# A layer with 32 routed experts: both up products of a quad of experts in a row on TensorE, the neighbours' gather and scatter behind them

## The chip, the core and the metric

The kernel runs on one core of a Trainium2 chip. Times are device microseconds of that core; the time of a kernel is the median of several runs. One further execution was taken by the hardware profiler, and all rows in this document come from such an execution. Its engines are called TensorE (PE in the rows; PEld are its weight loads), VectorE (DVE), ScalarE (ACT), GpSimd (POOL) and SyncE (SP), whose queue issues the loads.

## The reference

One decoder layer for 256 tokens of width 1024, in float32: a mixer (differential attention, an mLSTM, gates and an output projection), then a mixture of experts, then a norm. The change is in the experts, which the reference computes densely:

```python
gate = (one_hot(g_sel, N_GROUPS)[:, :, None] * w_e[:, None, :] * p_grp[:, None, None])
for gi in range(N_GROUPS):                       # 4 groups of 8 experts
    a = jnp.einsum('td,edf->tef', t, w_e1[gi])   # 1024 -> 256
    b = jnp.einsum('td,edf->tef', t, w_e3[gi])   # 1024 -> 256
    hid = jax.nn.silu(a) * b * gate[:, gi, :, None]
    y = y + jnp.einsum('tef,efd->td', hid, w_e2[gi])   # 256 -> 1024
```

Each token has two experts with a gate other than zero. The layer's result is x + gt2 * y, and a norm over it is the output.

## The kernel before, in words

The mixer takes the first 250 us or so. Then comes the expert loop. It works on quads of 4 experts, 8 quads in all (`NQ`), each expert on at most 32 tokens (`CAP`), so that a quad's 4 x 32 token places fill the 128 rows of a matmul's output. The loop body is written for 4 quads (`LOOP`) and runs twice. A second block with the same body would handle experts with more than 32 tokens; it is skipped for these inputs. In the rows a float32 matmul of the program stands as two records, so 32 matmuls are x64.

For each quad TensorE does this (function `quad` of the tensor block, lines 1550 to 1568):
- `up("w1")`, line 1533: four experts side by side in four column groups of the array, into the left half of `up_bank`. It first waits until all four w1 tiles have landed (`arrived`, line 1524).
- `gather(0)`, line 1507: matmuls with a one-hot matrix that pick the tokens of the *next* quad, first half of the 1024 features, into `token_bank`.
- `scatter`, line 1496: adds the *previous* quad's outputs to the four banks of y, by a matrix of gates.
- `gather(1)`, line 1507: the second half of the features, into the same `token_bank`. It waits until the first half is evacuated.
- `up("w3")`, line 1533: the second up product, into the right half of `up_bank`.
- `turn`, lines 1514 and 1517: transposes of the next quad's gate matrix and of this quad's hidden values, into `token_bank` again. It waits for the second half's evacuation (`g_evac`) and for the hidden values (`hid_done`).
- `down`, line 1545: experts 0 and 1, then 2 and 3, each pair waiting for its two w2 tiles.

ScalarE (function `quad` of the scalar block, lines 643 to 647) evacuates the two gathers (`gather_half`, line 639, four activations each, then `g_evac`) and computes the sigmoid of the w1 product (line 647). The sigmoid waits on `used` until all 8 up tiles of the quad are consumed, so until the w3 product is done. VectorE multiplies it with both products (lines 1103 and 1105, `hid_done`), copies the transposes (1108, 1110), scales the output (1114, `o_dve`) and makes the next one-hot matrices (1092, 1095).

The weights come by SyncE's queue in the order of use: four tiles of w1, four of w3, four of w2, each 1 MB, so 12 MB a quad. There are 16 slots (`ring` has 12, the buffers hT, qkT, gm and mqk are four more), numbered in turn. SyncE issues load number m once tile m - 16 is consumed (`used`, incremented by the last matmul on each tile). So w3 of a quad goes to the slots of the quad before's w1, w2 to those of its w3, and w1 to those of w2 two quads before.

After the loop TensorE scatters the last quad's output (line 1496), ScalarE squares (668), VectorE norms (1149), and SyncE stores (376).

Of the kernel before, what the change touches and what calls it, by code (L numbers as in the profile page):

```python
# [20 lines left out]
ACT = mybir.ActivationFunctionType  # L21
# [7 lines left out]
G, E, F = 4, 8, 256  # L29
# [54 lines left out]
UP_UNITS = 8  # L84
QU = len(QUAD_UNITS)
# [50 lines left out]
def build(nc, t, out):  # L136
    with ExitStack() as ctx:
# [3 lines left out]
        def sem(name):  # L141
            return ctx.enter_context(nc.semaphore(name))
# [50 lines left out]
        sig, act_a, hid = tmp[:, 0, 0:F], tmp[:, 0, F:2 * F], tmp[:, 1, 0:F]  # L193
# [32 lines left out]
        def S(name, n=1):  # L226

            if name not in small:
                small[name] = (small_at[0], n)
                small_at[0] += n  # L230
            a, n = small[name]
            return sm[:, a:a + n]
# [21 lines left out]
        def pb(job):  # L254
            return bank[JOB[job] % 8]
# [17 lines left out]
        token_bank, up_bank, out_banks = pb("lg"), pb("gt2b0"), (pb("gt2b1"), pb("rank"))  # L273
# [6 lines left out]
        used = sem("used")  # L280
# [8 lines left out]
        s = {n: sem(n) for n in names}  # L289
# [102 lines left out]
        def _(act):  # L392
# [241 lines left out]
            def gather_half(b, half, count):  # L634

                act.wait_ge(s["g_full"], count)
                for j in range(4):
                    k = 4 * half + j
                    ins = act.activation(xg[:, b, k, :], token_bank[:, j * P:(j + 1) * P], ACT.Identity,  # L639
                                         bias=S("B2", KD)[:, k:k + 1], scale=S("A2", KD)[:, k:k + 1])  # L640
                ins.then_inc(s["g_evac"], 1)

            def quad(it, b):
                gather_half(1 - b, 0, it * 2 + 3)
                gather_half(1 - b, 1, it * 2 + 4)
                act.wait_ge(used, it * QU + UP_UNITS)
                act.activation(sig, up_bank[:, 0:F], ACT.Sigmoid).then_inc(s["sig_r"], 1)  # L647

            gather_half(0, 0, 1)
            gather_half(0, 1, 2)  # L650
            with act.Fori(0, NQ // 2) as i:
                for b in range(2):
                    quad(i * 2 + b, b)
            act.wait_ge(s["flag_r"], 1)
            over = act.value_load(flag[0:1, 0:1], min_val=0, max_val=1)
            with act.If(over > 0):
                with act.Fori(1, PASSES) as p:
                    with act.Fori(0, NQ // 2) as i:
                        for b in range(2):
                            quad(p * NQ + i * 2 + b, b)  # L660
# [493 lines left out]
        def _(pe):  # L1154
# [137 lines left out]
            for h in range(HEADS):  # L1292
                for c in range(2):
                    ps = take(f"s{2 * h + c}")
                    r = slice(64 * c, 64 * c + 64)
# [196 lines left out]
            def scatter(b, stop):  # L1492

                for tt in range(TT):
                    for c in range(2):
                        ins = pe.matmul(y_banks[2 * tt + c][:], ptg[:, b, tt, :], outs2[:, 512 * c:512 * c + 512],  # L1496
                                        start=False, stop=stop, skip_group_check=True)
                    if stop:
                        ins.then_inc(s["y_full"], 1)
                return ins  # L1500

            def gather(half):

                for j in range(4):
                    k = 4 * half + j
                    for tt in range(TT):
                        ins = pe.matmul(token_bank[:, j * P:(j + 1) * P], xn[:, tt, k * P:(k + 1) * P],  # L1507
                                        pone[:, tt].rearrange("p a n -> p (a n)"), start=(tt == 0), stop=(tt == TT - 1))
                ins.then_inc(s["g_full"], 1)

            def turn(with_hidden):

                for tt in range(TT):
                    ins = pe.transpose(token_bank[:, tt * P:(tt + 1) * P], pgate[:, tt].rearrange("p a n -> p (a n)"), ident)  # L1514
                if with_hidden:
                    for f in range(2):
                        ins = pe.transpose(token_bank[:, T + f * P:T + (f + 1) * P], hid[:, f * P:(f + 1) * P], ident)
                ins.then_inc(s["pt_full"], 1)

            def arrived(w, e, r, j):  # L1520

                m = j * QU + QUAD_POS[(w, e)]
                n = NPRE + m % XSLOTS
                pe.wait_ge(landed[slot_of(n)], r * (16 * TURNS) + (landed_value(n) + 16 * (m // XSLOTS)))
                return unit(n, 2 if w == "w2" else 8)

            def up(w, r, j, b):

                half = slice(0, F) if w == "w1" else slice(F, 2 * F)
                wt = [arrived(w, e, r, j) for e in range(QUAD)]  # L1530
                for k in range(KD):
                    for e in range(QUAD):
                        ins = pe.matmul(up_bank[e * CAP:(e + 1) * CAP, half], xg[:, b, k, e * CAP:(e + 1) * CAP],  # L1533
                                        wt[e][:, k, :], start=(k == 0), stop=(k == KD - 1), tile_position=(0, e * CAP))
                        if k == KD - 1:
                            ins.then_inc(used, 1)

            def down(r, j):

                for pair in ((0, 1), (2, 3)):  # L1540
                    wt = {e: arrived("w2", e, r, j) for e in pair}
                    for c in range(2):
                        for f in range(2):
                            for e in pair:
                                ins = pe.matmul(out_banks[c][e * CAP:(e + 1) * CAP, :], hidT[:, f, e * CAP:(e + 1) * CAP],  # L1545
                                                wt[e][:, f, 512 * c:512 * c + 512], start=(f == 0), stop=(f == 1),
                                                tile_position=(0, e * CAP))
                                if c == 1 and f == 1:
                                    ins.then_inc(used, 1)

            def quad(r, j):
                it, b = r * LOOP + j, j % 2
                pe.wait_ge(s["g_evac"], it * 2 + 2)
                pe.wait_ge(s["hid_done"], it + 1)
                up("w1", r, j, b)
                pe.wait_ge(s["pg_ready"], it + 2)
                pe.wait_ge(s["pt_evac"], it + 2)
                gather(0)
                pe.wait_ge(s["o_dve"], it + 1)
                scatter(1 - b, False).then_inc(s["scat"], 1)  # L1560
                pe.wait_ge(s["g_evac"], it * 2 + 3)
                gather(1)
                up("w3", r, j, b)
                pe.wait_ge(s["g_evac"], it * 2 + 4)
                pe.wait_ge(s["hid_done"], it + 2)
                turn(True)
                pe.wait_ge(s["hT_evac"], it + 1)
                down(r, j)
# [22 lines left out]
            with pe.Fori(0, NQ // LOOP) as r:  # L1591
                for j in range(LOOP):
                    quad(r, j)
            pe.wait_ge(s["flag_r"], 1)
            over = pe.value_load(flag[0:1, 0:1], min_val=0, max_val=1)
            with pe.If(over > 0):
                with pe.Fori(1, PASSES) as p:
                    with pe.Fori(0, NQ // LOOP) as r:
                        for j in range(LOOP):
                            quad(p * (NQ // LOOP) + r, j)  # L1600
# [26 lines left out]
```

## Time and profile before

| | us |
|---|---|
| median of 3 timed runs | 538.76 (537.51 to 539.1) |
| span of the profiled execution | 540.9 |
| TensorE busy in it | 442.4 (82%) |
| ScalarE, VectorE, GpSimd busy | 171.8, 161.4, 140.9 |
| mean granted TensorE clock | 0.920 |
| moved by DMA | 163.16 MB, mean 302 GB/s |

The page gives the profiled execution's time as its span, 540.9 us; that is 2.1 us above the median of the timed runs. Busy shares are averages over stages with different limits: GpSimd is busy in the mixer only, and the expert loop begins at 289.5 us, when TensorE starts the first w1 product. Of TensorE's busy time, the up products (line 1533) and the down products (line 1545) are the loop's large items.

### The profile page before, as it was taken

What the parts mean: (1) busy time and instruction counts of PE and PEld (TensorE: products, weight loads), DVE (VectorE), ACT (ScalarE), POOL (GpSimd) and SP (SyncE); (2) the same over time, 40 slices, a digit from 0 to 9 for tenths busy, and PEclk for the clock granted to TensorE, in tenths of its full rate; (3) what the DMA queues carried; (4) which work ended last, traced back from release to release, by engine and by line L of the source; (5) the groups of instructions that cost most, each with busy time, mean ns of one, the idle gap of its engine ahead of it and who ended that gap; (6) DMA issues with size and microseconds to landing.
All of it is one profiled execution on the core that took longest, in us unless ns stands there. A gap on an engine that the chain in (4) does not pass through costs nothing.

```text
span 540.9 us, 8837 instructions
## 1 busy us (share of the span) xinstructions
PE 442.4 (82%) x3772; PEld 324.9 (60%) x3772; DVE 161.4 (30%) x338; ACT 171.8 (32%) x305; POOL 140.9 (26%) x36
## 2 busy tenths in 40 slices
PE   2656998999999999979969898969848588385783
PEld 0325988899899999969846453616225153151431
DVE  0245105796464331682360111120111101102013
ACT  3044523743495485433343212301203012030122
POOL 0019663665556559745000000000000000000000
PEclk9857999998999999988989898988979989799898
DMA  8999689396794464579599999999999999999972
GB/s 299 383 370 382 174 270 349 116 366 218 219 355 166 148 229 170 167 260 291 186 397 325 366 376 349 393 350 361 381 348 389 354 355 388 348 383 359 352 293 81
DMA packets 116742, 163.16 MB, mean 302 GB/s; under 512 B 6642, under 2 KB 99044, under 8 KB 116580
## 3 DMA queue, kind: packets, MB, share of 16 engines
q1 hardware_dynamic: 111968, 159.53, 86.0%
q10 hardware_dynamic: 4740, 3.15, 2.1%
q8 instruction: 25, 0.41, 0.3%
q14 instruction: 9, 0.07, 0.0%
HBM read 161.61 MB, written 1.05 MB: 301 GB/s over the span
## 4 chain that ended last, share of the span: by engine, by line
PE 71%; DMA 15%; DVE 7%; ACT 2%; SPq 2%; issue 2%; DVEq 0%
PE bank L1225 32%; PE bank L1533 12%; DMA ring<-in_w_e 9%; PE bank L1507 7%; PE bank L1545 6%; PE bank L1496 5%; DMA ring<-in_w_ada 4%; PE bank L1178 2%; DMA mqk<-in_w_e 2%; DVE gm L971 2%; SPq L337 1%; DVE hT_r L762 1%; PE bank L1579 1%; PE bank L1462 1%; PE bank L1514 1%
## 5 line engine op out<-in xcount | busy, mean ns | idle before, releaser
L387 POOL TENSOR_TENSOR ring_r<-ring,ring_r 128x2048 fp32r<-128x2048 f32 x30 | 140.6, 4695 | 114.0 <-ACT ring_r L419 114.0
L1225 PE MATMUL bank<-ring_r 128*128 128x256 f32 x832 | 115.0, 291 | 4.7 <-ACT ring_r L587 2.9
L1225 PEld LDWEIGHTS bank<-ring_r 128*128 128x128 f32 x832 | 108.0, 198 | 7.3 <-issue 3.8
L639 ACT ACTIVATE raw<-bank,sm 128x128 f32<-128x128 f32 x72 | 27.1, 457 | 190.0 <-PE bank L1507 190.0
L1533 PE MATMUL bank<-ring,raw 128*32 128x256 f32 x768 | 51.0, 417 | 29.3 <-DMA ring<-in_w_e 28.9
L419 ACT ACTIVATE ring_r<-ring 128x2048 fp32r<-128x2048 f32 x30 | 57.3, 1910 | 43.8 <-PE bank L1225 28.7
L1533 PEld LDWEIGHTS bank<-ring,raw 128*32 128x32 f32 x768 | 27.9, 120 | 50.9 <-issue 38.5
L1103 DVE TENSOR_TENSOR tmp<-bank,tmp 128x256 f32<-128x256 f32 x8 | 3.4, 424 | 147.5 <-ACT tmp L647 147.5
L1545 PE MATMUL bank<-ring,WT 128*32 128x512 f32 x192 | 42.6, 676 | 3.6 <-DVE WT L1108 3.5
L1507 PEld LDWEIGHTS bank<-const,xn 128*128 128x128 f32 x288 | 35.4, 197 | 8.8 <-issue 7.3
L1178 PE MATMUL bank<-ring,sm 128*32 128x256 f32 x384 | 27.4, 432 | 13.9 <-DMA ring<-in_w_ada 13.9
L1507 PE MATMUL bank<-const,xn 128*128 128x128 f32 x288 | 37.2, 284 | 1.1 <-DVE const L1054 1.1
L1225 PE MATMUL bank<-hT_r,ring_r 128*128 128x256 f32 x256 | 36.1, 283 | 0.0
L1496 PE MATMUL bank<-v,const 128*128 128x512 f32 x72 | 32.5, 593 | 1.7 <-DVE sm L1134 1.7
L1225 PEld LDWEIGHTS bank<-hT_r,ring_r 128*128 128x128 f32 x256 | 33.3, 193 | 0.0
L1545 PEld LDWEIGHTS bank<-ring,WT 128*32 128x32 f32 x192 | 11.0, 122 | 31.2 <-issue 28.2
L1178 PEld LDWEIGHTS bank<-ring,sm 128*32 128x32 f32 x384 | 12.2, 120 | 26.0 <-DMA ring<-in_w_ada 11.3
L1114 DVE TENSOR_TENSOR v<-bank,att 128x512 f32<-128x512 f32 x16 | 10.3, 686 | 56.0 <-PE bank L1545 56.0
L1533 PE MATMUL bank<-hT,raw 128*32 128x256 f32 x64 | 16.4, 408 | 8.4 <-DMA mqk<-in_w_e 8.4
L1496 PEld LDWEIGHTS bank<-v,const 128*128 128x128 f32 x72 | 13.0, 190 | 15.5 <-issue 15.5
L1225 PE MATMUL bank<-raw_r,ring_r 128*128 128x256 f32 x128 | 17.8, 281 | 0.0
L1533 PE MATMUL bank<-qkT,raw 128*32 128x256 f32 x64 | 16.4, 408 | 0.0
(296 smaller groups left out, 530.5 us busy)
## 6 DMA issues: line engine op xcount, KB each, us to landing
ring<-in_w_e SPq DMA_DIRECT2D x72, 1024.0 KB, 12.0
ring<-in_w_ada SPq DMA_DIRECT2D x24, 1024.0 KB, 11.4
ring<-in_w_in SPq DMA_DIRECT2D x22, 1024.0 KB, 8.1
hT<-in_w_e SPq DMA_DIRECT2D x6, 1024.0 KB, 11.9
qkT<-in_w_e SPq DMA_DIRECT2D x6, 1024.0 KB, 12.0
gm<-in_w_e SPq DMA_DIRECT2D x6, 1024.0 KB, 13.0
mqk<-in_w_e SPq DMA_DIRECT2D x6, 1024.0 KB, 12.7
ring<-in_w_out SPq DMA_DIRECT2D x4, 1024.0 KB, 5.2
```

Source lines behind the costliest of these rows:

```text
L337: sp.dma_start(unit(n, 2), w_ada[:, k0:k0 + 2, i * D:(i + 1) * D]).then_inc(landed[slot_of(n)], 16)
L387: pool.tensor_tensor(ring_r[:, slot_of(n), :], ring[:, slot_of(n), :], hi(d).bitcast(F32), ALU.subtract).then_inc(s["w_lo"], 1)
L419: act.activation(hi(d), ring[:, slot_of(n), :], ACT.Copy).then_inc(s["w_hi"], 1)
L639: ins = act.activation(xg[:, b, k, :], token_bank[:, j * P:(j + 1) * P], ACT.Identity, bias=S("B2", KD)[:, k:k + 1], scale=S("A2", KD)[:, ...
L971: own(dve.tensor_tensor(va, va, view, ALU.add), "merged", i + 1)
L1114: ins = dve.tensor_tensor(outs2[:, sl], out_banks[c][:], gt2b[:, sl], ALU.mult)
L1178: ins = pe.matmul(ps[32 * u:32 * u + 32, 0:256], S("cs", 8)[:, k:k + 1].to_broadcast([P, 32]), w[:, k - k0, 256 * u:256 * u + 256], start= ...
L1225: ins = pe.matmul(out, left(k), right(k), start=(i == 0 and k == 0), stop=(i == 2 and k == nk - 1))
L1496: ins = pe.matmul(y_banks[2 * tt + c][:], ptg[:, b, tt, :], outs2[:, 512 * c:512 * c + 512], start=False, stop=stop, skip_group_check=True)
L1507: ins = pe.matmul(token_bank[:, j * P:(j + 1) * P], xn[:, tt, k * P:(k + 1) * P], pone[:, tt].rearrange("p a n -> p (a n)"), start=(tt == ...
L1533: ins = pe.matmul(up_bank[e * CAP:(e + 1) * CAP, half], xg[:, b, k, e * CAP:(e + 1) * CAP], wt[e][:, k, :], start=(k == 0), stop=(k == KD ...
L1545: ins = pe.matmul(out_banks[c][e * CAP:(e + 1) * CAP, :], hidT[:, f, e * CAP:(e + 1) * CAP], wt[e][:, f, 512 * c:512 * c + 512], start=(f ...
```

## The change

On TensorE the w3 product is issued right behind the w1 product, ahead of the gathers and the scatter. On ScalarE the sigmoid goes ahead of the two evacuations, since its input is now complete first. The waits themselves stay the same, each with the instruction it belonged to.

```diff
@@ scalar block @@
             def quad(it, b):
+                act.wait_ge(used, it * QU + UP_UNITS)
+                act.activation(sig, up_bank[:, 0:F], ACT.Sigmoid).then_inc(s["sig_r"], 1)
                 gather_half(1 - b, 0, it * 2 + 3)
                 gather_half(1 - b, 1, it * 2 + 4)
-                act.wait_ge(used, it * QU + UP_UNITS)
-                act.activation(sig, up_bank[:, 0:F], ACT.Sigmoid).then_inc(s["sig_r"], 1)
@@ tensor block @@
                 up("w1", r, j, b)
+                up("w3", r, j, b)
                 pe.wait_ge(s["pg_ready"], it + 2)
                 pe.wait_ge(s["pt_evac"], it + 2)
                 gather(0)
...
                 scatter(1 - b, False).then_inc(s["scat"], 1)
                 pe.wait_ge(s["g_evac"], it * 2 + 3)
                 gather(1)
-                up("w3", r, j, b)
                 pe.wait_ge(s["g_evac"], it * 2 + 4)
                 pe.wait_ge(s["hid_done"], it + 2)
                 turn(True)
```

TensorE's instructions at the first quad of the loop body, before (raw is the tile of gathered tokens, const holds the one-hot and gate matrices, xn the tokens, v the quad's output, WT the transposed hidden values; REGISTER_ALU and ISA rows belong to waits):

```order
L1524 ISA
L1524 REGISTER_ALU
L1533 MATMUL bank<-ring,raw 32x256 x32
L1556 REGISTER_ALU
L1507 MATMUL bank<-const,xn 128x128 x8
L1496 MATMUL bank<-v,const 128x512 x4
L1561 REGISTER_ALU
L1507 MATMUL bank<-const,xn 128x128 x8
L1533 MATMUL bank<-ring,raw 32x256 x32
L1564 REGISTER_ALU
L1514 MATMUL bank<-const 128x128 x2
L1517 MATMUL bank<-const,tmp 128x128 x2
```

The same place on TensorE after the change:

```order
L1524 ISA
L1524 REGISTER_ALU
L1533 MATMUL bank<-ring,raw 32x256 x64
L1557 REGISTER_ALU
L1507 MATMUL bank<-const,xn 128x128 x8
L1496 MATMUL bank<-v,const 128x512 x4
L1562 REGISTER_ALU
L1507 MATMUL bank<-const,xn 128x128 x8
L1564 REGISTER_ALU
L1514 MATMUL bank<-const 128x128 x2
L1517 MATMUL bank<-const,tmp 128x128 x2
```

The second group of 32 up matmuls has joined the first, and the transposes now stand directly behind the second gather.

ScalarE's instructions at the head of the loop body, before (one body here holds two quads; raw is what an evacuation writes, tmp what the sigmoid writes):

```order
L651 ISA
L639 ACT_TABLE_LOAD
L639 ACTIVATE raw<-bank,sm 128x128 x4
L636 REGISTER_ALU
L639 ACTIVATE raw<-bank,sm 128x128 x4
L646 ISA
L647 ACT_TABLE_LOAD
L647 ACTIVATE tmp<-bank 128x256
```

And after the change:

```order
L651 ISA
L645 ACT_TABLE_LOAD
L645 ACTIVATE tmp<-bank 128x256
L636 ISA
L639 ACTIVATE raw<-bank,sm 128x128 x4
L636 REGISTER_ALU
L639 ACTIVATE raw<-bank,sm 128x128 x4
```

The sigmoid stands ahead of both evacuations, and of the two table loads per body one is left. VectorE, GpSimd and SyncE issue the same instructions in the same order.

## Rows read from the trace of the kernel before

**Rows 1.** The page: span, and DMA busy tenths in 40 equal slices of it.
```profile
span 540.9 us, 8837 instructions
...
DMA  8999689396794464579599999999999999999972
```

**Rows 2.** Busy time by stretches, all engines: stretch, its length, busy us, clock, DMA share.
```profile
314.00:338.00 24.00, 21.89 (x210) 11.30 (x206) 3.62 (x9) 4.67 (x10) 0.00 (x0) 0.93 1.08 356
...
434.40:468.70 34.30, 23.78 (x204) 12.10 (x204) 3.65 (x8) 4.68 (x10) 0.00 (x0) 0.90 1.08 366
```

**Rows 3.** Waits from 270 us on: us in total, times, longest.
```profile
ACT raw L639 <- PE bank L1507: 190.0, 18, 24.9
...
PE bank L1533 <- DMA ring<-in_w_e: 28.9, 4, 8.4
...
PE bank L1514 <- DVE tmp L1105: 12.7, 8, 1.6
```

**Rows 4.** Chain of waits, last quad: start, us, engine or DMA, line.
```profile
490.84 12.14 DMA ring<-in_w_e
...
503.11 4.91 PE bank L1533 x64
508.02 1.98 PE bank L1507 x16
510.00 3.44 PE bank L1496 x8
513.44 1.78 PE bank L1507 x16
515.23 3.71 PE bank L1533 x64
...
519.83 0.43 DVE tmp L1105
...
520.40 0.41 PE bank L1514 x2
...
521.55 3.63 PE bank L1545 x16
...
525.28 3.65 PE bank L1545 x16
528.96 0.05 DVE v L1114
```

**Rows 5.** Line 349, loads issued from 502.9 to 503.4 us (w3's last two).
```profile
L349 SPq DMA_DIRECT2D ring<-in_w_e x2: 2921/2922/2922, 500.1 to 503.1; - x2
...
DMA to landing us min/median/max: 11.9/11.9/12.0
```

**Rows 6.** Order of time, ScalarE, last quad: the second gather's evacuation.
```profile
515.26 1.50 ACT L639 ACTIVATE raw<-bank,sm 128x128 f32<-128x128 f32 x4 [3.72 <-PE bank L1507]
```

**Rows 7.** Order of time: VectorE behind quad 5's down product; SyncE's queue for quad 7.
```profile
460.41 1.29 DVE L1114 TENSOR_TENSOR v<-bank,att 128x512 f32<-128x512 f32 x2 [7.06 <-PE bank L1545]
...
477.80 28.17 SPq L349 DMA_DIRECT2D ring<-in_w_e  x7
```

**Rows 8.** Busy time by stretches, line 1533 (up products) alone.
```profile
365.00:371.00 6.00, 5.35 (x64) 3.29 (x64) 0.72 1.10 348
...
503.00:508.50 5.50, 4.91 (x64) 2.63 (x64) 0.75 1.10 348
300.00:304.20 4.20, 3.66 (x64) 1.98 (x64) 1.00 1.10 356
```

**Rows 9.** Busy time by stretches, line 1545 (down products) alone.
```profile
354.00:362.00 8.00, 7.05 (x32) 1.63 (x32) 0.79 1.10 349
...
521.00:529.00 8.00, 7.25 (x32) 1.88 (x32) 1.00 0.33 130
```

**Rows 10.** DMA from 285 to 300 us (40 slices), and SyncE's waits, 285 to 360.
```profile
GB/s 358 350 358 350 350 347 347 347 350 352 350 347 350 347 347 350 350 350 347 350 350 350 281 180 104 175 101 238 336 385 382 401 371 325 358 270 303 366 360 374
...
SPq L349 <- PE bank L1533: 18.7, 6, 6.2
```

## The prediction

> **What bounds the kernel now.** I began with the top of the page: the span and the DMA line [rows 1]. Every other number below is to be read inside that span, and the DMA line reads 9 in all slices from the 21st to the 38th (271 to 514 us), which is nearly the whole expert loop. The second view was busy time by stretches [rows 2]. A quad in the middle of the loop takes 34.3 us (from one w1 product's start to the next) while TensorE is busy for only 23.8 of them and the DMA share is 1.08. So the loop from its fourth quad on lasts as long as its 12 MB of weights need to arrive, and TensorE has more than 8 us per quad to give away. The list of waits says the same from the other side [rows 3]: TensorE's long waits are at the up product (line 1533), for a load, and the longest is 8.4 us.
>
> That would make any order on TensorE free, so the third view has to be the chain of waits at the end of the loop, in order of time [rows 4], because the last quad has no transfer behind it that could hide anything. There the reader should see four things. The w1 product starts at 503.11, after its load. Gather, scatter, gather fill 508.02 to 515.22. The w3 product starts at 515.23. The down product's second pair starts at 525.28. Beside this stand the landings [rows 5]: the last w3 load is issued at 503.1 and lands 12.0 us later, at about 515.1. So the two gathers and the scatter (7.20 us) lie exactly in the time in which TensorE would otherwise wait for w3, and they cost nothing. After the last w3 has landed, TensorE has only an up product, the turn and the down product to do, and it is just done with the first down pair when the last w2 is there.
>
> **The change, part by part.** No matmul, activation or weight load is added or removed (only one of ScalarE's two table loads per pair of quads goes, and both stood where it waits anyway: 190 us in 18 times for TensorE [rows 3]). Two things move.
>
> ScalarE: the sigmoid goes ahead of the two evacuations of the gathers. It needs the w3 product, and the gathers now stand behind that product on TensorE, so it delays nothing. The sigmoid, VectorE's two products and their hand-over made TensorE wait 1.59 us at line 1514 in each quad (12.7 us in 8 times [rows 3]). That wait goes, since 7.20 us of gather and scatter now lie over it. What is late in its place is the second gather's evacuation. The turn writes the same bank (token_bank) and waits for g_evac; before, the w3 product (3.71 us) covered that evacuation, now nothing does. It takes 1.50 us [rows 6], starts 0.04 us behind the gather (515.26 against 515.22), and the hand-over to TensorE is 0.14 as for VectorE (the chain's last VectorE step before the turn ends at 520.26, the turn starts at 520.40). That is 1.68 in place of 1.59: nothing gained.
>
> TensorE: the w3 product moves ahead of gather, scatter, gather. In the quads whose weights are all there (the first three) it only changes the order of the same work. They keep their 24 us (TensorE is busy for 21.9 in such a stretch [rows 2]), and I cost them at 0.1 each (1.68 for 1.59), hidden by the wait that follows. In a quad that is bound by loads, TensorE runs the w1 product, then waits for w3 (12 us behind w1), and then has everything else to do. From a w3 product's start to the end of the quad I count 5.35 + 7.20 + 1.68 + 1.15 + 5.37 = 20.75 us (terms below), and 3.7 for the next w1 product: 24.5 us, against the 34.3 us until the next w3. So the middle quads stay at the pace of the loads. Nor does a later release of w2's slots hold up a load: quad 5's w2 is read by 460.4 now, would be read some 7 us later, and the slots are wanted from 477.8 on [rows 7].
>
> In the last quad the cost is laid bare. Counted from the w3 product's start at about 515.2, which is set by a landing that does not move:
> - The w3 product. It now follows a wait of about 8.3 us, as the w1 product did. Behind such waits the up product took 4.91 to 5.35 us at a mean granted clock of 0.70 to 0.75 in five quads, against 3.66 with the clock at 1.00 throughout [rows 8]. I take 5.35, the top, because one of the five rows already shows it. Bounds: 3.66 (no slow part), and twice that, 7.3 (all of it at the lower of the two clock levels).
> - Gather, scatter, gather: 1.98 + 3.44 + 1.78 = 7.20 [rows 4].
> - The evacuation in the open with its hand-over: 1.68.
> - The turn, hidden's transposes, VectorE's copy and the steps between: 520.40 to 521.55, 1.15 [rows 4].
> - The down product. Before, the last pair waited for its w2 until 525.2, and the product took 7.4 us to VectorE's start at 528.96. In the new order all of w2 has long landed. The third quad is such a case: 7.05 us in a stretch of 8 us with a mean clock of 0.79 [rows 9]. With only the two levels 1.2 and 2.4 GHz, 0.79 means 42% of 8 us, 3.4 us, at the lower one, which cost half of that, 1.7. Without the drop it is 7.05 - 1.68 = 5.37. I take 5.37, since the five later down products ran at 1.00, as that of the last quad [rows 9]. Bounds 5.37 and 7.4.
>
> Sum: 20.75 us from the w3 product's start, against 528.96 - 515.23 = 13.73 before: 7.0 us more. The output part behind it (closing scatter, norm, stores) is unchanged. The sum is made inside the profiled execution: 540.9 becomes 547.9. The median of the timed runs, 538.76, is 2.1 us below the profiled span, so I carry over the difference and not the span: 538.76 + 7.0 = 545.8 us.
>
> **A rule of the Trainium skill against the trace.** The rows on the up product [rows 8] show a clock below 1.00 only right behind a wait of several us. The page "TensorE: Matmul & The Clock Gate", section "HAM oscillation — how this bites in real kernels", advises to do a tile's matmuls in one stretch ahead of the DMA wait, so that the engine stays at its high clock. Read that way, w1 and w3 back to back would both run at 3.66, and the sum would be 7.0 - 1.69 = 5.3. The trace speaks against it: the w3 load is 12 us behind w1, so the instructions stand back to back while the work does not. It is a rival below.
>
> **The rivals.**
> 1. The clock drops during the last quad's down product too, as it did in the first three quads (mean 0.79 in the third [rows 9]), or the w3 product runs longer at the lower level. For it: where w2 was all there, the down product was at that pace three times of three. Against it: those three followed TensorE's 1.59 us wait closely, and the five down products of the later quads kept 1.00. Time: 5.37 becomes 7.05, +8.7, 547.5 us.
> 2. TensorE keeps the high level through the wait for w3. For it: the w1 product runs just ahead of the wait. Against it: a like wait of 8.4 us cost it in every quad. Time: +5.3, 544.1 us.
> 3. The loads hide it and nothing changes: 538.8 us. For it: DMA share 1.08 and 8.4 us of waiting per quad. Against it: what is hidden in quads 0 to 6 has no next load to hide behind in the last; it would need some 7 us of slack after the last w3 lands, and the chain shows none.
> 4. Faster. w3's slots come free 7.2 us earlier in the first quads, so the stream of loads might move ahead. For it: the queue shows a hole of about 2 us (104 and 101 GB/s against 350) near 294, and SyncE waited 18.7 us for line 1533 in the first quads [rows 10]. Against it: the load issued at that hole (293.12) wants w1's first slot, and w1 is read at the same time as before; behind it the row reads 336 to 401 but for three short dips to 270 at the least, so there is no second hole to close. It wins only if the last w3 lands over 7 us earlier, by 508.2. If all of the 18.7 us went into the stream: 538.8 + 7.0 - 18.7 = 527.1 us.
> 5. Slots of w2 freed later starve the stream in mid-loop. By [rows 7] there are some 10 us to spare, so it needs a much longer down phase. Each us beyond them costs up to one per quad: 550 us or more.
>
> **How the numbers follow.** Chances: forecast 0.61, rival 1 0.23, rival 2 0.07, rival 3 0.04, rival 4 0.02, rival 5 0.03. About 0.3% (1.6 us) is what a measurement of this kernel can tell from no change, so faster 0.02, same 0.04, slower 0.94. The range takes in rival 2 just about, +5.1, and rival 1 with one further us, +9.7: 543.9 to 548.5. The cases of no change and of starved loads are left out, together under 0.1; the rest of what is left out is the spread inside the cases.
>
> **What would show it right or wrong.** In the changed profile: TensorE's wait for DMA in the middle quads of 8.2 to 8.4 us stands between w1 and w3, not ahead of w1. The last w3 product starts 12 us behind the last w1's landing and lasts 4.9 to 5.7 us. Line 1514 waits 1.6 us for ScalarE's line 639 and not for VectorE. The down product of the last quad lasts 5.4 us, or 7.05 with a clock below 1. VectorE's line 1114 starts 20.5 to 21 us after the last w3 product. The stream's last load lands at the same time as before, within 0.5 us, and the mean quad keeps 34.3. The prediction is wrong if the last w3 product starts much before 515, if a middle quad takes longer than 34.5, or if the gathers run during the wait after all.

## The result, and the profile after

| | before | after |
|---|---|---|
| median of timed runs, us | 538.93 (4 runs) | 548.75 (544.42 to 551.69, 4 runs) |
| ratio to before, 95% interval | | 1.0164 (1.0094 to 1.0233) |
| the same in a later job (experiment 1) | | 1.0135 (1.0091 to 1.0180) |
| span of the profiled execution, us | 540.9 | 546.9 |
| start of the last w3 product to line 1114, us | 13.73 | 20.59 |

The kernel became slower, by 8.8 us of 538.9 in the first job (5.1 to 12.6) and by 7.3 us of 542 in the second (4.9 to 9.8), both worked out from the ratio; the two medians of the first job lie 9.8 us apart. Some executions of every kernel are some 10 us longer than its others, and the ratios leave them out. The forecast was 7.0 us more. From trace to trace the last quad accounts for 6.9 us, as the rest of this section shows.

The page of the changed kernel, span and DMA line, stands against [rows 1]:

```profile
span 546.9 us, 8833 instructions
...
DMA  8999579596994375498799999999999999999912
```

The DMA line again reads 9 from the 21st to the 38th slice and then falls to 1, where it fell to 7 before: the stretch at the end in which next to nothing is loaded and the kernel is not yet done has become longer. Busy time by stretches for a quad in the middle (answers to [rows 2]):

```profile
433.70:468.00 34.30, 22.26 (x204) 12.17 (x204) 3.90 (x10) 4.67 (x10) 0.00 (x0) 0.90 1.08 367
```

A quad still takes 34.3 us (the w3 products of the quads start at 445.76, 480.08 and 514.42, by the chain of waits), at the same DMA share of 1.08. The waits from 270 us on, against [rows 3]:

```profile
ACT tmp L645 <- PE bank L1533: 168.1, 8, 25.6
...
PE bank L1533 <- DMA ring<-in_w_e: 39.4, 8, 8.4
...
PE bank L1533 <- DMA mqk<-in_w_e: 15.5, 3, 8.4
...
PE bank L1514 <- ACT raw L639: 12.8, 8, 1.6
```

ScalarE's long waits now stand at the sigmoid (line 645), since it comes first. TensorE's waits for loads at line 1533 became more, 54.9 us in 11 times: in a middle quad 8.4 us between the w1 and the w3 product, and a further 1.3 to 1.7 us ahead of w1. Line 1514 no longer waits for VectorE but for ScalarE's evacuation (line 639), 12.8 us in 8 times where it was 12.7. So the one wait took the place of the other at the same price. Now the chain of waits in the last quad, against [rows 4]:

```profile
502.43 11.86 DMA ring<-in_w_e
...
514.42 5.16 PE bank L1533 x64
519.58 1.98 PE bank L1507 x16
521.56 3.44 PE bank L1496 x8
525.00 1.80 PE bank L1507 x16
...
528.38 0.44 PE bank L1514 x2
...
529.07 0.44 DVE WT L1108
...
529.55 5.43 PE bank L1545 x32
535.01 0.06 DVE v L1114
```

The reader should see that after the last weight load of the up products (502.43 plus 11.86) everything stands in one row: the w3 product, gather, scatter, gather, the evacuation (526.82 to 528.38), turn, down. The load takes as long from issue to landing as in [rows 5], within 0.1 us:

```profile
L349 SPq DMA_DIRECT2D ring<-in_w_e x2: 2922/2922/2922, 499.5 to 502.4; - x2
...
DMA to landing us min/median/max: 11.8/11.8/11.9
```

The up and down products alone, by stretches (first line 1533, then line 1545), against [rows 8, 9]:

```profile
445.00:451.50 6.50, 5.36 (x64) 2.80 (x64) 0.67 1.03 409
480.00:486.00 6.00, 5.27 (x64) 2.73 (x64) 0.72 1.03 410
514.00:520.00 6.00, 5.16 (x64) 2.71 (x64) 0.71 1.03 410
```

```profile
461.00:467.00 6.00, 5.38 (x32) 1.42 (x32) 1.00 1.10 347
495.00:501.00 6.00, 5.38 (x32) 1.42 (x32) 1.00 1.10 347
529.00:535.50 6.50, 5.38 (x32) 1.42 (x32) 1.00 0.01 3
```

The w3 product behind the wait takes 5.16 to 5.36 us at a mean clock of 0.67 to 0.72. The down product, with all of w2 landed and the clock at 1.00, takes 5.38 us. Line 1114 starts at 535.01 against 528.96, 6.05 us later. That is 20.59 - 13.73 = 6.86, less 0.81 by which the last w3 product started sooner in this execution (514.42 against 515.23). This 0.81 is a balance: the loop's first w1 product started 2.4 us sooner (287.11 against 289.48), the loads of the loop took 1.7 us longer, and before the gathers ended 0.1 us later than the last w3 tile would have let its product start. Behind line 1114 both executions need 11.9 us.

### The profile page after: what moved, and what is told of

Read it like the earlier page. It is cut to its first block, busy times and chain, and to the rows that moved or that the text cites. A ratio compares the mean times of both kernels' runs of the same rounds, so it can differ in the third digit from the quotient of the medians.

```text
span 546.9 us, 8833 instructions
## 1 busy us (share of the span) xinstructions
PE 431.4 (79%) x3772; PEld 323.6 (59%) x3772; DVE 165.2 (30%) x338; ACT 166.6 (30%) x301; POOL 141.0 (26%) x36
## 4 chain that ended last, share of the span: by engine, by line
PE 68%; DMA 17%; DVE 6%; ACT 3%; SPq 3%; issue 2%; DVEq 0%; ACTq 0%
PE bank L1225 31%; DMA ring<-in_w_e 9%; PE bank L1533 9%; PE bank L1545 8%; PE bank L1507 7%; PE bank L1496 5%; DMA mqk<-in_w_e 4%; DMA ring<-in_w_ada 4%; PE bank L1178 2%; DVE gm L971 2%; ACT raw L639 2%; SPq L349 1%; SPq L337 1%; DVE hT_r L762 1%; PE bank L1579 1%
## 5 line engine op out<-in xcount | busy, mean ns | idle before, releaser
L1225 PE MATMUL bank<-ring_r 128*128 128x256 f32 x832 | 112.7, 288 | 4.7 <-ACT ring_r L587 2.9
L1225 PEld LDWEIGHTS bank<-ring_r 128*128 128x128 f32 x832 | 105.7, 195 | 7.3 <-issue 3.8
L1533 PE MATMUL bank<-ring,raw 128*32 128x256 f32 x768 | 52.6, 423 | 39.9 <-DMA ring<-in_w_e 39.4
L1533 PEld LDWEIGHTS bank<-ring,raw 128*32 128x32 f32 x768 | 30.4, 122 | 62.1 <-issue 52.5
L645 ACT ACTIVATE tmp<-bank 128x256 f32<-128x256 f32 x8 | 3.1, 384 | 168.1 <-PE bank L1533 168.1
L1178 PE MATMUL bank<-ring,sm 128*32 128x256 f32 x384 | 27.5, 434 | 13.1 <-DMA ring<-in_w_ada 13.1
L1545 PE MATMUL bank<-ring,WT 128*32 128x512 f32 x192 | 33.8, 612 | 3.5 <-DVE WT L1108 3.5
L1533 PE MATMUL bank<-hT,raw 128*32 128x256 f32 x64 | 18.5, 448 | 15.5 <-DMA mqk<-in_w_e 15.5
L1178 PEld LDWEIGHTS bank<-ring,sm 128*32 128x32 f32 x384 | 12.2, 120 | 25.4 <-DMA ring<-in_w_ada 10.8
L1545 PEld LDWEIGHTS bank<-ring,WT 128*32 128x32 f32 x192 | 9.1, 112 | 24.0 <-issue 21.0
L1108 DVE COPY WT<-bank 128x256 f32<-128x256 f32 x8 | 3.4, 425 | 64.5 <-PE bank L1517 64.5
## 6 DMA issues: line engine op xcount, KB each, us to landing
hT<-in_w_e SPq DMA_DIRECT2D x6, 1024.0 KB, 11.9
gm<-in_w_e SPq DMA_DIRECT2D x6, 1024.0 KB, 12.8
mqk<-in_w_e SPq DMA_DIRECT2D x6, 1024.0 KB, 12.7
```

The lines of the kernel that those rows point to most:

```text
L1178: ins = pe.matmul(ps[32 * u:32 * u + 32, 0:256], S("cs", 8)[:, k:k + 1].to_broadcast([P, 32]), w[:, k - k0, 256 * u:256 * u + 256], start= ...
L1225: ins = pe.matmul(out, left(k), right(k), start=(i == 0 and k == 0), stop=(i == 2 and k == nk - 1))
```

## The experiments

Where a kernel below has quads 3 and 7 in another order, that is because the loop body holds four quads and runs twice. Ratios are to the kernel before, run in the same job.

### 1. The changed kernel again

No edit.

> The changed kernel once more, unaltered. Theory (tail): the change costs only in the last quad, where the step from the last w3 product's start to VectorE's scaling of the output (line 1114) grew from 13.7 to 20.6 us between the two profiles. So 20.6 us again from trace to trace, whatever the whole time is, and against the kernel before between 5 and 8 us. Rival (stream): the 9.8 us between the medians hold a second cost of 2 to 4 us in the first three quads, where the stream of loads fell back by 1.7 us in the changed kernel's profile (from the issue of load 16 to the landing of load 95: 232.0 us before, 233.7 after). Then the difference stays at 8 to 11 us and the stream takes 233.5 or more again.

Measured: ratio 1.0135 (1.0091 to 1.0180), 7.3 us. The chain of waits in the last quad:

```profile
515.13 5.79 PE bank L1533 x64
...
530.89 5.43 PE bank L1545 x32
536.35 0.06 DVE v L1114
```

From the w3 product's start to line 1114 it is 21.22 us, of which 5.79 is the w3 product. So 20.6 was at the low end, and the spread between the two executions is the part of the w3 product that ran at the lower clock (a mean of 0.63 over 6 us here, 0.71 there). The stream of loads took 232.5 us from load 16's issue to load 95's landing (of the loads 0 to 95, load 16 is the first that needs a slot to come free), not 233.7: the rival's mark was not met, though it is 0.5 us over the kernel before.

### 2. The old order in quads 3 and 7 only

```diff
 # scalar block, body of four quads
+                if j < 3:
+                    sigmoid()
                 gather_half(1 - b, 0, it * 2 + 3)
                 gather_half(1 - b, 1, it * 2 + 4)
+                if not (j < 3):
+                    sigmoid()
 # tensor block
                 up("w1", r, j, b)
+                if j < 3:
+                    up("w3", r, j, b)
...
                 gather(1)
+                if not (j < 3):
+                    up("w3", r, j, b)
```

> Quads 0 to 2 and 4 to 6 in the changed order on TensorE and ScalarE, quads 3 and 7 (the last of each loop body) in the order before. Tail theory: the last quad is as it was, w3's start to line 1114 is 13.7 us, the time is that of the kernel before within 1 us (539 to 540). Rival (stream, or any cost in the middle): the six quads in the changed order keep their share, 2 us or more over the kernel before.

Measured: ratio 1.0023 (0.9978 to 1.0068). The chain (line numbers are 8 higher here: 1541 is the up product, 1553 down, 1122 the scaling):

```profile
514.37 3.75 PE bank L1541 x64
...
520.74 7.44 PE bank L1553 x32
...
528.20 0.06 DVE v L1122
```

13.83 us, as before (13.73). Six of eight quads run in the new order and the cost is gone to within the interval. That interval reaches 3.7 us, so it does not exclude the rival's 2 us; the stream of loads took 233.9 us in this execution, 1.8 more than before.

### 3. The new order in quads 3 and 7 only

The same edit with the conditions `j == 3` and `not (j == 3)`.

> The complement: only quads 3 and 7 in the changed order, the other six as before. Tail theory: the whole cost is there, 20.6 us from w3's start to line 1114 in the last quad, 6 to 7 us over the kernel before. Rival (stream): less than the changed kernel by 2 us or more, since quads 0 to 2, in which the loads were delayed, are as before.

Measured: ratio 1.0114 (1.0059 to 1.0169), 6.2 us. The chain:

```profile
515.75 5.81 PE bank L1541 x64
...
531.54 5.43 PE bank L1553 x32
...
536.99 0.06 DVE v L1122
```

21.24 us. Behind quad 3 come quads that wait for their loads anyway, so its order is hidden (the stream of loads took 232.4 us here and 232.0 before); behind quad 7 comes nothing. The step in the last quad alone is 7.5 us longer than before, as much as the whole time grew, within the interval (3.2 to 9.2). Together 2 and 3 place the cost in the last quad, but for what the intervals leave open.

### 4. Only the second gather behind w3

```diff
                 gather(0)
                 pe.wait_ge(s["o_dve"], it + 1)
                 scatter(1 - b, False).then_inc(s["scat"], 1)
+                up("w3", r, j, b)
                 pe.wait_ge(s["g_evac"], it * 2 + 3)
                 gather(1)
```

(w3's old place is taken out, and ScalarE's sigmoid stands between the two evacuations.)

> All quads: w1 product, first gather, scatter, w3 product, second gather, turn, down; on ScalarE the sigmoid between the two evacuations. So 5.4 of the 7.2 us stay in the wait for w3 and 1.8 move behind it. Tail theory in its sharper form (the end is the last landing of w2 plus one pair of the down product): the down product may start up to 1.8 us later than before, since its second pair waits until 525.2 anyway; with 1.8 (gather) + 0.1 (evacuation in place of the hand-over of the hidden values) it starts at about 523.4, its second pair follows four steps behind, and the time is that of the kernel before within 0.7 us. Rival (each us of TensorE's work that moves behind the last w3 costs a us): 1.9 us over the kernel before.

Measured: ratio 1.0010 (0.9977 to 1.0043). The chain:

```profile
514.97 3.66 PE bank L1533 x64
518.63 2.00 PE bank L1507 x16
...
523.39 5.43 PE bank L1545 x32
528.84 0.06 DVE v L1114
```

The down product starts at 523.39, 1.84 us later than in [rows 4], and yet line 1114 starts at 528.84, 13.9 us behind the w3 product. Down's two pairs overlap when their weights are there (5.43 us in one piece), and before they could not, as the last w2 landed at about 525.2. So the first 1.8 us moved behind w3 are free, and only what goes beyond is paid. The rival's 1.9 us did not show in the trace (13.87 us against 13.73); the ratio's interval, up to 2.3 us, would not exclude it. The w3 product stood here behind a wait of 1.7 us, not 8.4, and kept 3.66 us. This splits the cost of the whole change: of 7.22 us of gathers and scatter 5.4 lie beyond the free 1.8, and the w3 product at the lower clock adds 1.5 (5.16 for 3.71) to 2.1 us (experiments 1 and 3).

### 5. The wait for w3 filled

```diff
                 up("w1", r, j, b)
+                if j == 3:
+                    for _ in range(18):
+                        pe.matmul(up_bank[:, F:2 * F], ident, xn[:, 0, 0:F], start=True, stop=True)
                 up("w3", r, j, b)
```

> The changed kernel, and in quads 3 and 7 between the w1 and the w3 product 18 further matmuls (128 x 128 by 128 x 256, float32) into the half of up_bank that the w3 product then overwrites from its first step. At the pace of the other 128 x 256 matmuls of this kernel they take some 7 to 8 us, in a wait of 8.3. Theory: that wait costs nothing but the clock behind it, so the last w3 product takes 3.66 us at a clock of 1.00 in place of 5.16 and 5.79 in the two profiles so far, the step from its start to line 1114 falls from 20.6 and 21.2 to 19.0 us or so, and the time is 1.5 to 2 us below the changed kernel's. Rival (the up product is slow there since it reads tiles that landed last, or since loads share the memory with it): it stays at 5.2 to 5.8 us with TensorE busy ahead of it, and nothing is gained.

Measured: ratio 1.0137 (1.0072 to 1.0202), no gain in the time. By stretches, the last w3 product (line 1533) and then the last down product (line 1545):

```profile
511.00:516.00 5.00, 3.66 (x64) 2.39 (x64) 1.00 1.03 407
```

```profile
525.00:533.00 8.00, 7.05 (x32) 1.62 (x32) 0.79 0.02 4
```

The first half of the theory holds: 3.66 us at 1.00, so it is the clock and nothing about the tiles that makes the product slow behind the wait. But the clock now fell in the down product, which took 7.05 in place of 5.38, and the step to line 1114 was 20.8 us. What was gained was given back later, by the mechanism of the first rival. That the filling brought this about is not shown: quad 3 of the same execution has the same filling and the same waits (0.4, 1.6 and 0.5 us), and its down product kept the clock:

```profile
386.00:394.00 8.00, 5.38 (x32) 1.42 (x32) 1.00 1.10 351
```

### 6. ScalarE's old order with TensorE's new one

```diff
             def quad(it, b):
-                act.wait_ge(used, it * QU + UP_UNITS)
-                act.activation(sig, up_bank[:, 0:F], ACT.Sigmoid).then_inc(s["sig_r"], 1)
                 gather_half(1 - b, 0, it * 2 + 3)
                 gather_half(1 - b, 1, it * 2 + 4)
+                act.wait_ge(used, it * QU + UP_UNITS)
+                act.activation(sig, up_bank[:, 0:F], ACT.Sigmoid).then_inc(s["sig_r"], 1)
```

> TensorE's new order alone; ScalarE keeps the order before (both evacuations, then the sigmoid). Theory: behind the second gather now stand in a row the evacuation (1.54 us), the sigmoid (0.4) and VectorE's two products with the hand-over (1.0), 3.0 us in place of 1.68, so the step from w3's start to line 1114 is 1.3 us longer than in the changed kernel, 21.9 to 22.5 us. The time is that of the changed kernel plus 1.3 us. Rival (ScalarE's order is of no account, since the gathers and the scatter hide the sigmoid in either): the step stays at 20.6 to 21.2.

Measured: ratio 1.0187 (1.0134 to 1.0240). The profiled execution has a span of 557.7 us and its loop begins 6 us later, so only steps inside a quad are read from it. The chain:

```profile
521.94 5.54 PE bank L1533 x64
...
532.89 1.80 PE bank L1507 x16
...
536.22 0.28 ACT tmp L647
...
537.55 0.41 PE bank L1514 x2
...
538.70 7.10 PE bank L1545 x32
...
545.82 0.06 DVE v L1114
```

From the second gather's end (534.69) to the turn (537.55) it is 2.9 us in place of 1.6, as expected. The step to line 1114 is 23.9 us and not 21.9 to 22.5, because the down product took 7.10 (a mean clock of 0.77 over 7.5 us). That the longer wait ahead of it brought the clock down is not shown: in quads 3 and 5 of the same execution the wait was 2.9 us as well and the down product took 5.38 us at 1.00. Behind the 4.3 us of quads 4 and 6, where a table load stands in the wait, the clock fell both times (a mean of 0.79 over 8 us). In the step of 2.9 us for 1.6 ScalarE's half of the change shows its worth: without it TensorE's half would cost 1.3 us more.

### 7. Both waits filled

```diff
                 gather(1)
+                if j == 3:
+                    for _ in range(3):
+                        pe.matmul(out_banks[0][:, 0:F], ident, xn[:, 0, 0:F], start=True, stop=True)
```

(on top of the edit of experiment 5)

> The kernel with the filled wait (changed order, 18 further matmuls ahead of the w3 product in quads 3 and 7), and besides three further matmuls behind the second gather in these quads, into an output bank that the down product overwrites from its first step; they take 1.3 us of the 1.62 in which TensorE waits for the evacuation. In the kernel with only the first filling the w3 product took 3.66 us, but the granted clock fell in the down product, which took 7.10 in place of 5.38, so the step from w3's start to line 1114 was 20.8 us. Theory (the fall there came from TensorE's wait just ahead of the turn): the down product takes 5.4 us again and the step is 19.0 to 19.1 us, 1.5 us under the changed kernel's 20.6. Rival (it comes by chance, whatever TensorE does before): 7.1 us again, or in no order with the filling.

Measured: the chain (w3, then down), and the down product by stretches:

```profile
514.23 3.66 PE bank L1533 x64
...
527.86 5.43 PE bank L1545 x32
```

```profile
527.50:533.50 6.00, 5.38 (x32) 1.42 (x32) 1.00 0.02 5
```

3.66 and 5.38 us, both at 1.00, and line 1114 starts 19.1 us behind the w3 product, as the theory had it. But the theory's rival, that the fall in the down product comes by chance, stands: quad 3 in experiment 5 kept 5.38 us without this second filling, and so did the last quads of the change and of experiments 1 and 3 without any. In the whole time a gain is not seen: the ratio is 1.0153 (1.0100 to 1.0207), and an interval 5.8 us wide can't tell 1.5 us. In this execution the stream of loads took 234.8 us, 2.8 more than before; part of that may be the filling in quad 3.

### 8 and 9. The old order, with the last load in two halves

Experiment 4 says that the end is the last landing plus what is left to do then. This tests that from the other side, on the kernel before.

```diff
+                if j == LOOP - 1 and u == QU - 1:
+                    sp.dma_start(dst[:, 0:1, :], expert[:, 0:1, :]).then_inc(landed[i], 16)
+                    sp.dma_start(dst[:, 1:2, :], expert[:, 1:2, :]).then_inc(s["last_half"], 16)
+                    return
...
+                    if j == LOOP - 1 and pair == (2, 3):
+                        for f in range(2):
+                            if f == 1:
+                                pe.wait_ge(s["last_half"], r * 16 + 16)
+                            for c in range(2):
+                                for e in pair:
...
```

> The kernel before (old order), but the very last w2 tile of each loop body (expert 3 of quads 3 and 7) is loaded as two halves of 0.5 MB, by row halves f, with a semaphore each, and the second down pair of these quads runs f by f (both column halves of f = 0 first). Theory: the end is the last landing plus what TensorE has left to do then. The first half should land 1.3 us ahead of the second (0.5 MB at 409 GB/s), so half of the second pair (1.7 us of 3.65) is done by the last landing or soon after, and the step from the last landing to line 1114 falls from 3.8 us to 2.2 to 2.5. The time is 1.3 to 1.6 us below the kernel before, too little for more than the trace to show surely. Rival (a split load lands later, by its second issue or its smaller pieces): the last landing moves back by as much as is gained, and line 1114 starts where it did.

Measured: no ratio from this job (the next run has one). In order of time on TensorE and VectorE (1563 is the first down pair, 1553 the second, 1119 the scaling):

```profile
521.14 0.59 PE L1553 MATMUL bank<-gm,WT 128*32 128x512 f32 x1
...
524.15 0.59 PE L1553 MATMUL bank<-gm,WT 128*32 128x512 f32 x1
```

```profile
524.82 1.29 DVE L1119 TENSOR_TENSOR v<-bank,att 128x512 f32<-128x512 f32 x2 [5.64 <-PE bank L1553]
```

The first half is there at 521.0, the second at 522.3 (issued at 508.69, 13.6 us to landing). The second pair starts on the first half, and line 1119 starts 2.6 us after the last landing in place of 3.8. From the last w3 tile's landing to it are 12.7 us in place of 14.0.

> The kernel with the last load of quads 3 and 7 in halves, unaltered, once more: in the first job the step from the landing of the last w3 tile to VectorE's scaling of the output was 12.7 us in place of 14.0, but too few undisturbed runs were there for a ratio. Theory: 12.7 us again, and a ratio to the kernel before of 0.995 to 0.999 (1.2 us of 540 is 0.23%). Rival (the gain is given back behind line 1119 or in the mixer): a ratio of 1.000 or more, with the step at 12.7.

Measured: ratio 0.9974 (0.9927 to 1.0021). It is the only kernel here below the one before, and the interval does not exclude no change. The step was 13.1 us, not 12.7. The chain tells why:

```profile
487.28 12.23 DMA ring<-in_w_e
...
499.64 5.99 PE bank L1538 x64
505.64 1.98 PE bank L1512 x16
...
512.84 3.71 PE bank L1538 x64
```

In this execution the w1 product behind the wait took 5.99 us, so gather, scatter and gather ended at 512.8, 1.3 us after the last w3 had landed (511.5). The cover that the old order has is tight. The last w3 lands 12.0 us behind the last w1, and 7.2 of these go to the gathers and the scatter, so an up product of 4.8 us fits (each product starts 0.14 us behind its landing); 4.91 is 0.1 too long [rows 4], and 5.99 is 1.2 too long.

## Why the prediction was right

The time lies 3.0 us over the forecast of 545.8 by the medians, and 548.75 is just over the upper end of 548.5; by the two ratios (8.8 and 7.3 us) the cost of 7.0 is inside both intervals. In the trace, step by step:

- **What bounds the kernel.** Right. The middle quads kept 34.3 us in the new order (experiment 2), and the cost is in the last one (experiment 3), but for a possible 1.5 us in the first quads (below), which the sum did not have.
- **The w3 product, 5.35.** 5.16 in the changed kernel, 5.79 and 5.81 in experiments 1 and 3. The bounds (3.66 and 7.3) hold; I had taken the top of five rows for an end, and it was nearer to the middle: two of three products lay over the 5.7 us that I had named as the most. Experiments 5 and 7 (3.66 us at 1.00) show that the clock is the cause.
- **Gather, scatter, gather, 7.20.** 7.22.
- **The evacuation in the open, 1.68.** 1.58, from the second gather's end (526.80) to the turn (528.38); the hand-over took 0.04 and not VectorE's 0.14. That it takes the place of the wait for the hidden values, at the same price, is right; experiment 6 shows what it would have been with ScalarE's old order (2.9).
- **Turn to down, 1.15.** 528.38 to 529.55, 1.17.
- **The down product, 5.37.** 5.38 of busy time, and 5.46 from its start to line 1114, which is what the sum should have held. It had not been seen at the full clock with all weights landed; the estimate took 1.7 us off a row at a mean clock of 0.79.
- **The sum, 20.75.** 20.59, and 21.22 and 21.24 in experiments 1 and 3, just over the 20.5 to 21 that I had named.
- **The loads.** That the last landings come at the same time was right within 0.7 us (load 95 at 524.45 against 525.15) in part by luck: this execution's loop began 2.4 us earlier, and its stream of loads took 1.7 us longer.
- **The waits.** The 8.4 us between w1 and w3 came, but some 1.5 us of wait stayed ahead of w1.

The first rival (the clock falls in the last down product as well) did not come in the changed kernel's three relevant executions (the change, experiments 1 and 3) but did in experiments 5 and 6, at 1.7 us as priced. What decides it the runs do not show. The row that the rival rested on, the down product at 0.79 in the first three quads, is itself no rule: experiment 3 has the same order there, and its first three quads ran at 1.00, the second as follows:

```profile
329.00:337.00 8.00, 5.38 (x32) 1.42 (x32) 1.00 1.09 349
```

The second rival, that the w3 product keeps the high clock, came only where TensorE had work in the long wait (experiments 5 and 7) or where the wait was short (experiment 4). The Trainium skill's page "TensorE: Matmul & The Clock Gate", section "HAM oscillation — how this bites in real kernels", describes a loop in which each wait for a load lets the clock fall, so that the next tile's matmuls start at the lower one. The trace agrees with that: 5.16 to 5.81 us behind the wait of 8.4 us, 3.66 with the wait filled. Its advice, which the prediction cites, is to do the tiles' work ahead of the wait; here w3's work could not be done ahead of it, since its tiles had not landed. The third rival (the loads hide it) is excluded by experiments 1 and 3, the fourth (faster) and fifth (starved loads, 550 us or more) did not come.

One point stays open. The stream of loads, from load 16's issue to load 95's landing, took 232.0 us in the kernel before, and with the first quads in the old order or that of experiment 4 it took 232.0 to 232.4 (experiments 3, 4, 8 and 9). With the w3 product ahead of the gathers in the first quads it took 233.7, 232.5 (experiment 1), 233.9 (experiment 2), 233.0 (experiments 5 and 6) and 234.8 (experiment 7). The two groups do not overlap, though each number is one execution. So the change seems to cost about 1.5 us more at the start of the loop, in the traces of the change and of experiment 2 near loads 17 and 21; the ratio of experiment 2 leaves room for it, and 1.2 us there and 6.2 us in experiment 3 add up to about the 7.3 of experiment 1. This is the reverse of the fourth rival: load 20, which waits for w3's first slot, was issued 7.4 us behind load 16 and not 10.8, and the stream still took longer. What delays it was not tried.

## What to carry to other kernels

In a loop that is bound by loads, ask of each piece of work between two loads whether it stands in a wait, and read the last pass apart: it is the only one in which a wait lost is not made up. What may stand behind the last landing is what needs that landing's data; gathers for other quads belong ahead of it. A move is free as far as the slack to the next landing reaches, here 1.8 us of 7.2.

## What the runs showed that I had not expected

- The down product, behind waits of no more than 1.6 us, ran at 1.00 (5.38 us) or at a mean of 0.79 (7.05 us), in quads 3 and 7 of one execution (experiment 5) with the same waits ahead of them. So one trace of either kind proves nothing about a cure, experiment 7's included.
- Two pairs of column groups overlap in the down product when both have their weights: 5.38 us, against 3.63 and 3.65 one after the other when the second has to wait for its load.
- The up product right behind a wait of 8 us varied from 4.91 to 5.99 us in the last quad, at mean clocks of 0.75 to 0.60. Inside an execution it is regular: the w3 product shortened by about 0.1 us from quad to quad, 5.55, 5.46, 5.36, 5.27, 5.16 in the changed kernel and 6.18, 6.09, 5.99, 5.89, 5.79 in experiment 1. The executions differ by an offset, so a row of one execution tells the step to the next quad but not the level; this alone moves the end of the kernel by up to a microsecond.
